# Twelve projection groups multiply activations and their remainders in one 512-column product, and ScalarE and VectorE add the two halves

## The reference, cut to what matters

```python
h = _rmsnorm(x, g_mix[l])
(sb_q, sb_k, sb_v, ...) = jnp.split(h @ w_in[l], offsets, axis=-1)     # group sbq
...
h = _rmsnorm(x, g_ffn[l])
u = _causal_dwconv(h @ w_up[l], ff_conv_w[l], ff_conv_b[l])            # groups up0 to up10
u_val, u_gate = jnp.split(u, 2, axis=-1)
x = x + (jax.nn.silu(u_gate) * u_val) @ w_down[l]                      # groups down0, down1
```

## Time and profile before

| | |
|---|---|
| median of 3 runs | 995.21 us (995.01 to 996.04) |
| the profiled execution's own time | 997.04 us |
| its span, first to last instruction | 995.2 us |
| mean granted TensorE clock | 0.996 |
| TensorE busy | 983.3 us, 99% of the span |
| VectorE busy | 672.6 us, 68% |
| ScalarE busy | 593.6 us, 60% |
| chain of waits that ended last | 94% TensorE |

### The profile page before, as it was taken

How to read it: one execution, slowest core, us unless ns; L and a number is a source line. 1 busy time by engine, 2 the same in 40 slices (tenths; PEclk the granted TensorE clock), 3 DMA queues, 4 the chain that set the end, 5 groups by cost and what they waited for, 6 DMA issues and landing times.

```text
span 995.2 us, 18822 instructions
## 1 busy us (share of the span) xinstructions
PE 983.3 (99%) x8050; PEld 890.0 (89%) x8050; DVE 672.6 (68%) x896; ACT 593.6 (60%) x829; POOL 25.4 (3%) x26
## 2 busy tenths in 40 slices
PE   8999999999999999999999999999999999999996
PEld 7899987888989999998899999889899999987985
DVE  5675688867755788875556565785695556588565
ACT  7677576574537656654446676537754765654581
POOL 0000000000000000000000003000000000130000
PEclk9999999999999999999999999999999999999999
DMA  8762434656565665557654553553556446534331
GB/s 297 270 200 92 150 115 161 210 170 205 176 193 191 187 192 171 170 169 253 190 156 148 147 173 115 163 158 129 172 168 193 151 118 190 170 129 142 137 128 42
DMA packets 97283, 166.45 MB, mean 167 GB/s; under 512 B 6896, under 2 KB 32240, under 8 KB 96816
## 3 DMA queue, kind: packets, MB, share of 16 engines
q1 hardware_dynamic: 95792, 159.18, 50.7%
q0 software_dynamic: 976, 4.46, 1.3%
q10 hardware_dynamic: 432, 1.62, 0.4%
HBM read 164.19 MB, written 1.05 MB: 166 GB/s over the span
## 4 chain that ended last, share of the span: by engine, by line
PE 94%; DVE 2%; ACT 2%; issue 1%; DMA 1%; SPq 0%; DVEq 0%; ACTq 0%
PE proj L623 14%; PE proj L624 14%; PE proj L625 14%; PE proj L632 13%; PE proj L634 13%; PE proj L633 13%; PE mix L668 1%; PE mix L944 1%; PE mix L693 1%; PE mix L676 1%; PE mix L905 1%; PE mix L893 1%; DMA raw<-in_w_mem_kv 1%; ACT arena L1372 1%; PE mix L701 1%
## 5 line engine op out<-in xcount | busy, mean ns | idle before, releaser
L1532 DVE TENSOR_TENSOR wlo<-raw,whi 128x1024 fp32r<-128x1024 f32 (+2 forms) x304 | 356.6, 1202 | 177.3 <-ACT whi L1067 176.0
L1067 ACT ACTIVATE whi<-raw 128x1024 fp32r<-128x1024 f32 (+2 forms) x304 | 307.3, 1040 | 185.4 <-PE proj L634 81.3
L623 PE MATMUL proj<-act_hi,whi 128*128 128x256 f32 x1064 | 304.0, 286 | 0.5 <-ACT arena L1345 0.5
L624 PE MATMUL proj<-act_lo,whi 128*128 128x256 f32 x1064 | 301.0, 283 | 0.0
L625 PE MATMUL proj<-act_hi,wlo 128*128 128x256 f32 x1064 | 301.0, 283 | 0.0
L623 PEld LDWEIGHTS proj<-act_hi,whi 128*128 128x128 f32 x1064 | 203.2, 191 | 3.0 <-ACT arena L1345 1.4
L624 PEld LDWEIGHTS proj<-act_lo,whi 128*128 128x128 f32 x1064 | 203.3, 191 | 0.5
L625 PEld LDWEIGHTS proj<-act_hi,wlo 128*128 128x128 f32 x1064 | 203.2, 191 | 0.2
L632 PE MATMUL proj<-whi,y_hi 128*128 128x512 f32 (+1 forms) x340 | 133.3, 392 | 1.3 <-DVE wlo L1532 1.3
L634 PE MATMUL proj<-whi,y_lo 128*128 128x512 f32 (+1 forms) x340 | 132.3, 389 | 0.0
L633 PE MATMUL proj<-wlo,y_hi 128*128 128x512 f32 (+1 forms) x340 | 132.3, 389 | 0.0
(11 more groups left out here) (335 smaller groups left out, 1027.4 us busy)
## 6 DMA issues: line engine op xcount, KB each, us to landing
raw<-in_w_in SPq DMA_DIRECT2D x144, 512.0 KB, 4.4
raw<-in_w_up SPq DMA_DIRECT2D x88, 256.0 KB, 4.4
raw<-in_w_out SPq DMA_DIRECT2D x32, 512.0 KB, 3.5
raw<-in_w_down SPq DMA_DIRECT2D x22, 512.0 KB, 5.7
raw<-in_w_mem_k SPq DMA_DIRECT2D x8, 512.0 KB, 4.0
raw<-in_w_o SPq DMA_DIRECT2D x8, 512.0 KB, 3.9
raw<-in_w_mem_v SPq DMA_DIRECT2D x8, 512.0 KB, 4.1
raw<-in_w_mem_kv SPq DMA_DIRECT2D x7, 512.0 KB, 6.7
```

The lines of the kernel that those rows point to most:

```text
L623: mm(o, wh[:, i, wc], hi[:, k0 + i, :], start=begin and j % 2 == 0, stop=False, skip_group_check=True)
L624: mm(o, wh[:, i, wc], lo[:, k0 + i, :], start=False, stop=False, skip_group_check=True)
L1067: fn(whi[c % SPLIT][:, 0:w], raw[c % SLOTS][:, 0:w], ACT.Copy).then_inc(s.w_hi, 1)
L1532: tt(wlo[c % SPLIT][:, 0:w], raw[c % SLOTS][:, 0:w], f32(whi[c % SPLIT][:, 0:w]), ALU.subtract).then_inc(s.w_lo, 1)
```

## The change

`act_hi` and `act_lo` become the two halves of one tensor `act_both`. A new function `project_beside` streams both halves in one product of 512 columns against a block of `whi`, into one whole PSUM bank (columns 0 to 255 take hi by hi, columns 256 to 511 take lo by hi), and then the 256-column product of act_hi with `wlo` into columns 0 to 255. A triple of 256-column products becomes a pair. The two halves are added outside: ScalarE copies the upper half to SBUF (`one_side`), VectorE adds the lower half from PSUM to it (`both_sides`). It applies to sbq, up1 to up9 and hgq0 of both layers. A group now takes four banks: in the up stage `mix` for odd and all of `proj4` for even groups; for sbq and hgq0 their own two banks and `mix` banks 2 and 3. `proj` is now a view of `proj4`. ("..." marks what is left out.)

```diff
+SIDE_UP = tuple(f"up{c}" for c in range(1, FT // 2 - 1))
+SIDES = ((None, "sbq"), *((None, name) for name in SIDE_UP), *((L, "hgq0") for L in range(LAYERS)))
...
-        act_hi = sb("act_hi", [P, KT, SEQ], F32R)
-        act_lo = sb("act_lo", [P, KT, SEQ], F32R)
+        act_both = sb("act_both", [P, 2, KT, SEQ], F32R)
+        act_hi, act_lo = act_both[:, 0, :, :], act_both[:, 1, :, :]
...
-        proj = [ctx.enter_context(nc.psum_tensor(f"proj{i}", [P, NB, 512], F32)) for i in range(2)]
+        proj4 = ctx.enter_context(nc.psum_tensor("proj4", [P, 2 * NB, 512], F32))
+        proj = [proj4[:, NB * i:NB * i + NB, :] for i in range(2)]
...
+        def beside(name, L=None):
+
+
+            if name in SIDE_UP:
+                return [(mix if int(name[2:]) % 2 else proj4)[:, j, :] for j in range(4)]
+            return [bank(name, L)[:, 0, :], bank(name, L)[:, 1, :], mix[:, 2, :], mix[:, 3, :]]
...
+        FX = [ar(3072 + n * 1024, 4, SEQ) for n in range(2)]
...
+            def project_beside(name, L):
+
+                ps, at, out = shape[L, name], number[L, name], beside(name, L)
+                k0 = 0
+                for n, loads in enumerate(ps):
+                    pe.wait_ge(s.w_lo, at[n] + 1)
+                    k, cols = piece_dims(loads)
+                    wh = whi[at[n] % SPLIT][:, 0:k * cols].rearrange("p (k c) -> p k c", c=cols)
+                    wl = wlo[at[n] % SPLIT][:, 0:k * cols].rearrange("p (k c) -> p k c", c=cols)
+                    for j in range(4):
+                        wc = slice(j * P, (j + 1) * P)
+                        for i in range(k):
+                            begin, end = k0 + i == 0, k0 + i == KT - 1
+                            mm(out[j].rearrange("p (v t) -> p v t", v=2), wh[:, i, wc], act_both[:, :, k0 + i, :], start=begin, stop=False, skip_group_check=True)
+                            last = mm(out[j][:, 0:SEQ], wl[:, i, wc], act_hi[:, k0 + i, :], start=False, stop=end, skip_group_check=True)
+                    last.then_inc(s.w_used, 1)
+                    k0 += k
...
             project("xaq", None, act_hi, act_lo)
-            project("sbq", None, act_hi, act_lo)
+            pe.wait_ge(*out_of("xav", None))
+            project_beside("sbq", None)
 
             project("sbk", None, act_hi, act_lo, part=(0, 1))
             pe.wait_ge(s.xa_n, 1)
+            pe.wait_ge(*out_of("sbq", None))
...
             project("up0", None, act_hi, act_lo, ready=lambda k: pe.wait_ge(s.ffn_lo, k))
-            for c in range(1, FT // 2):
-                project(f"up{c}", None, act_hi, act_lo)
+            pe.wait_ge(*stage(6, None))
+            for c in range(1, FT // 2 - 1):
+                for name in ("memv",) if c == 1 else ("up0",) if c == 2 else (f"up{c - 2}",):
+                    pe.wait_ge(*out_of(name, None))
+                project_beside(f"up{c}", None)
+            project(f"up{FT // 2 - 1}", None, act_hi, act_lo)
             project("down0", None, y_hi, y_lo, ready=lambda k: pe.wait_ge(s.ff_l, (k + 1) // 2))
...
-                project("hgq0", L, act_hi, act_lo)
+                pe.wait_ge(*out_of("memout0", L))
+                project_beside("hgq0", L)
...
+            def one_side(to, name, L):
+
+                split_until(pieces_until(name, L))
+                act.wait_ge(*done(name, L))
+                if name in SIDE_UP:
+                    v = (mix if int(name[2:]) % 2 else proj4)[:, :, :]
+                    fn(to, v[:, :, SEQ:512], ACT.Copy).then_inc(s.side_in, 1)
+                else:
+                    for v, j in ((bank(name, L), 0), (mix[:, 2:4, :], 2)):
+                        last = fn(to[:, j:j + 2, :], v[:, :, SEQ:512], ACT.Copy)
+                    last.then_inc(s.side_in, 1)
...
-            leave("sbq", None, SBQK[:, 0:4, :])
+            one_side(SBQK[:, 0:4, :], "sbq", None)
...
             def hidden_gate(c):
-                act.wait_ge(*out_of(f"up{c}", None))
+                act.wait_ge(s.ff_v, c + 1)
                 fn(FU[c % 2][:, 2:4, :], FU[c % 2][:, 2:4, :], ACT.Silu).then_inc(s.ff_s, 1)
...
                 if c:
                     hidden_gate(c - 1)
                 split_until(pieces_until(name, None))
-                act.wait_ge(*done(name, None))
+                if name in SIDE_UP:
+                    one_side(FX[c % 2], name, None)
+                if c:
+                    hidden_upper(c - 1)
+                if name in SIDE_UP:
+                    act.wait_ge(*out_of(name, None))
+                else:
+                    act.wait_ge(*done(name, None))
                 if c >= 2:
                     act.wait_ge(s.ff_m, c - 1)
                 for j in range(4):
                     t = 2 * c + j % 2 + FT * (j // 2)
-                    last = fn(FU[c % 2][:, j, :], tiles(name)[:, j, :], ACT.Identity, scale=cols2[:, 2, t:t + 1], bias=cols2[:, 3, t:t + 1])
+                    x = FX[c % 2][:, j, :] if name in SIDE_UP else tiles(name)[:, j, :]
+                    last = fn(FU[c % 2][:, j, :], x, ACT.Identity, scale=cols2[:, 2, t:t + 1], bias=cols2[:, 3, t:t + 1])
                 last.then_inc(s.ff_c, 1)
-                if c:
-                    hidden_upper(c - 1)
...
+            def both_sides(to, name, L):
+
+                dve.wait_ge(s.side_in, SIDES.index((L, name)) + 1)
+                signal = out_of(name, L)[0]
+                if name in SIDE_UP:
+                    v = (mix if int(name[2:]) % 2 else proj4)[:, :, :]
+                    tt(to, v[:, :, 0:SEQ], to, ALU.add).then_inc(signal, 1)
+                else:
+                    for v, j in ((bank(name, L), 0), (mix[:, 2:4, :], 2)):
+                        last = tt(to[:, j:j + 2, :], v[:, :, 0:SEQ], to[:, j:j + 2, :], ALU.add)
+                    last.then_inc(signal, 1)
...
             split_until(pieces_until("sbq", None))
+            both_sides(SBQK[:, 0:4, :], "sbq", None)
             split_until(pieces_until("sbk", None))
...
                 if c:
                     hidden(c - 1)
                 split_until(pieces_until(name, None))
+                x = tiles(name)
+                if name in SIDE_UP:
+                    x = FX[c % 2]
+                    both_sides(x, name, None)
+                if c:
+                    hidden_lower(c - 1)
                 dve.wait_ge(s.ff_c, c + 1)
                 for d in (1, 2):
                     for j in range(4):
                         t = 2 * c + j % 2 + FT * (j // 2)
                         u = FU[c % 2][:, j, d:SEQ]
-                        last = stt(u, tiles(name)[:, j, 0:SEQ - d], cols2[:, 2 - d, t:t + 1], u, ALU.mult, ALU.add)
+                        last = stt(u, x[:, j, 0:SEQ - d], cols2[:, 2 - d, t:t + 1], u, ALU.mult, ALU.add)
                     if d == 1:
                         link(last)
-                last.then_inc(out_of(name, None)[0], 1)
-                if c:
-                    hidden_lower(c - 1)
+                last.then_inc(s.ff_v, 1)
+                if name not in SIDE_UP:
+                    dve.wait_ge(s.ff_v, c + 1)
+                    nc.vector.memset(stat[:, 245:246], 0.0).then_inc(out_of(name, None)[0], 1)
...
-                for name in ("hgq0", "uqa", "uqb", "uk", "uv"):
+                split_until(pieces_until("hgq0", L))
+                both_sides(HQT[:, 0:4, :], "hgq0", L)
+                for name in ("uqa", "uqb", "uk", "uv"):
                     split_until(pieces_until(name, L))
```

6 lines of the change are left out of this document (5 added, 1 removed).

## The result

The changed kernel takes 1008.94 us (median of 4 runs, 1008.18 to 1009.95) against 995.11 us of the kernel before on the same chip (4 runs): ratio 1.014, 95% interval 1.0125 to 1.0155. It is 13.8 us slower. The forecast was +12.7 us, 1007.9 us.

The account below looks back on a forecast made before the run. TensorE, busy 983.3 of 995.2 us, was taken to bound the kernel. Up stage +6.4, sbq +5.4, hgq0 -0.85 and clock +1.75 gave +12.7 us on 995.21, so 1007.9 us; 8-in-10 range 1002 to 1013.

Parts of the forecast that it names:

- What bounds the kernel: Whole kernel: TensorE, busy 983.3 of 995.2 us with no slack, so its work and waits set the time.
- sbq: QK transposes: TensorE waits 5.8 us for sums behind VectorE's four splits; +5.4 us net, bounds 5.2 and 5.6.
- The clock: At the sbq wait: idle TensorE falls to its lower clock once; +1.75 us, bounds 0 and 3.5.
- Rival (1): Whole kernel: the forecast without a fall of the clock, 1006.2 us; chance 0.27.
- rival (4): Up stage: waits of 1.66 us set the clock back too, 47 us over five groups, 1055 us; chance 0.05.
- The up stage: Up groups and down0: VectorE and ScalarE fall behind TensorE once the lead is gone; +6.4 us, bounds 3.4 and 7.6.
- the turn of 12.75 us: Up stage: ScalarE and VectorE's chain from SiLU to SiLU, without overlap, against TensorE's 11.09 us; range 12.35 to 12.9.
- TensorE's gain: Twelve changed groups: pairs of 0.3465 us replace triples of 0.360 us, saving 0.43 us a group, 5.2 us in all.
- hgq0: Both layers' hgq0: no wait or some 0.3 us, so -0.85 us in all, bounds -0.85 and 0.
- The sum: Whole kernel: up stage, sbq, hgq0 and clock terms add to +12.7 us, 1007.9 us; chance 0.55.
- rival (2): Whole kernel: up loop and sbq's sum stay hidden, so TensorE's 5.2 us are gained, 990.0 us; chance 0.05.
- (3): Up stage: turn of 11.4 us or less, covered by the lead, sbq wait as forecast; 997.6 us; chance 0.08.

Follow-up runs that it names:

- e6: Kernel of e2 with sbq's copy and sum moved ahead of the four splits, no instruction more or less; 995.54 us against 995.96, ratio 1.0.
- e8: Instructions of e1 in another order: VectorE's sum first, splits beside scale and bias, SiLU and rounding; 993.88 us against 995.96 before, ratio 0.9973.
- e2: The change in sbq alone, up groups and hgq0 as in the kernel before; 1000.79 us against 995.3, ratio 1.0054.
- e1: The change in up1 to up9 alone, sbq and hgq0 as in the kernel before; 1002.81 us against 995.3, ratio 1.0071.
- e5: Kernel of e2 plus 38 unread 256-column products ahead of the QK transposes, keeping TensorE busy; 1001.52 us against 995.96 before, ratio 1.0054.
- e4: The change in up1 to up3 alone, all other groups as in the kernel before; 995.09 us, ratio 0.9995.
- e11: Kernel of e9 with a piece's products grouped by width, 512, 512, 256, 256; 990.64 us against 995.52 before, ratio 0.9958.
- e3: The change in hgq0 of both layers alone, other groups as in the kernel before; 994.14 us against 995.3, ratio 0.9986.
- e9: All twelve groups changed, with the orders of e6 and e8 and the activation halves side by side; 992.8 us against 996.26 before, ratio 0.9969.

## Why the prediction was right, and which terms were off

**What bounds the kernel**: right. The two profiled spans differ mainly by what TensorE was made to wait, by its clock and by its products, and e6 and e8, which change nothing but places in two queues, move the whole kernel by 5.2 and 8.9 us against e2 and e1 (differences of the medians; 5.4 and 9.8 us by the ratios).

**sbq: +5.4 us forecast, +4.6 measured.** The mechanism is shown (e2, e6). The size was off by how early VectorE reached its splits, 0.7 us in this execution; the forecast took 58.38 from one execution and bounded the term at 5.2, as if that start were exact.

**The clock: +1.75 us forecast, +1.68 measured**, and +1.64 in e2. That the fall would come was right; that its size fits so well is in part luck. It was taken from the kernel's first products, and the profile grants these a clock of 1.00 (window 1.19 to 7.60 us), so that no row shows them slowed by the clock. Nor had the clock "stayed at the upper level" in the trace of before: near 178 us it fell while TensorE was busy (last section), which the slices of rows 1 hide. Rival (1), the same without a fall, is refuted by the windows. e5 shows in its trace that it goes away when TensorE has work. The Trainium skill ("TensorE: Matmul & The Clock Gate", section "The HAM clock gate") has an idle TensorE set back from 2.4 to 1.2 GHz; the windows agree, with 0.59 and 0.64 after 4.6 us of idleness. The waits of 1.4 to 1.6 us in the up stage, with which rival (4) would have brought 1055 us, left the clock up: 1.00 from 385 to 460 us.

**The up stage: +6.4 us forecast, +8.6 measured. This is the term that was mis-sized**, and the step of it that failed is the turn of 12.75 us. The mechanism holds: the splits in front of the sum, a lead that covers the first groups (e4), the first wait in group 6 instead of 5, then one in each group. The turn is 12.94 us.

The four scale-and-bias steps read SBUF now and take 2.08 us, not the 1.94 that the forecast took over from PSUM; those of up10, which still read PSUM, take 1.91 in the same trace. The taps were allowed to become cheaper from SBUF and didn't: 3.37 against 3.34 us. That makes 0.17 of the 0.19 us a turn, and over the eight turns between the first and the last SiLU 1.5 us. Another 0.4 us arose in the first turn, where ScalarE's copy had to wait 1.55 us for TensorE and VectorE 0.79 us for the copy, since up1 ended 0.4 us later than forecast, about half of it by the dearer pairs; the last 0.3 us are what is left for down0. The forecast's bounds gave the turn 0.4 us of room on the cheaper side and 0.15 on the dearer, too little: the stage cost more than its upper bound of 7.6 us.

The Trainium skill has a table for the place of the source that the forecast didn't use ("VectorE: DVE Perf Modes", section "The TRN2 errata"): it gives ScalarE 224 cycles of fixed cost from SBUF and 172 from PSUM, at 1.2 GHz. An estimate from that page is 0.043 us an instruction, 0.17 us for four; the trace has 0.14. The same table gives VectorE 58 cycles from SBUF and 120 from PSUM, by which eight taps would have become about 0.5 us shorter; the trace shows 0.03 us more, and the measurement decides.

**TensorE's gain: 0.43 us a group forecast, 0.22 measured in sbq and in the up groups** (0.353 us a pair in place of 0.3465), **0.41 in hgq0.** In the changed kernel this cost next to nothing, since VectorE's turn sets the stage there; it was what the reordered kernels lacked (e8: -1.9 us where -3.9 was forecast). The choice for it, two rows measured apart in streams of one width each, carried over to the alternating stream in hgq0 (0.3467) and not in the other ten groups, where grouping by width brings 0.348. No run shows why.

**hgq0: -0.85 us forecast, -0.83 measured** in two traces, and the median of e3 (-1.2 us, -2.3 to -0.4) agrees.

**The sum.** The misses +2.2 in the up stage and -0.8 at sbq have opposite signs, with some tenths elsewhere. So the total is nearer to the truth (+12.7 against +13.8) than its largest term, and that is luck. Rivals (2) and (3), a stage that stays hidden, are refuted for the kernel as it was changed; e11 reached the time of rival (2) with the order changed.

## What to carry to other kernels

When a step is moved off the engine that bounds the kernel, look up what stands in front of it in the other engines' queues: the same copy and sum cost 5.5 us behind four splits and nothing ahead of them (a wait of 1.0 us in e9). Where two engines hand work to each other several times a turn, add up the turn as a chain with the durations of the new operand places (SBUF or PSUM), and put work that nobody waits for into its gaps; a lead hides a turn that is too long only for some groups. And a price per product is good to a few nanoseconds only: the same pairs took 0.347 us in one place of the kernel and 0.353 in another.

## What the runs showed of the hardware, unexpected

**A fall of the clock without idleness.** TensorE of before by time, and windows of before; then the window of after in the same stage, which lies 6.5 us later there:

```profile
176.06 1.97 PE L790 MATMUL mix<-arena,const 4*128 4x256 f32 x8
...
178.00:180.00 2.00, 2.00 (x8) 1.63 (x8) 2.00 (x7) 1.97 (x3) 0.00 (x0) 0.75 0.93 326
180.00:182.00 2.00, 2.00 (x7) 1.51 (x6) 1.26 (x4) 1.99 (x2) 0.00 (x0) 0.50 1.02 392
```

```profile
186.00:188.00 2.00, 2.00 (x11) 1.63 (x10) 1.74 (x6) 1.97 (x3) 0.00 (x0) 1.00 1.03 365
```

TensorE is busy throughout in both (2.00 of 2.00 us), and yet before loses some 1.6 us here: the 40 digits of the page, each a 25 us average, hide it. Just ahead of the fall stand 2 us of products that use 4 of the 128 rows (`4x256`); they stand there in every execution, and the fall follows only in some. Of the 14 profiled executions six have it (before, e3, e4, e5, e6, e11), and these took 0.1 to 2.2 us more than the median of their kernel; the other eight took 0 to 1.7 us less. So it is a likely part of why runs of one kernel lie 2 to 3 us apart, and why this profiled execution took 997.04 us; the forecast took its 1.8 us over the median as mere scatter. What sets it off stays open.

**The same pair of products at two prices**: 512- and 256-column products that follow each other singly take 0.353 us a pair in sbq and in the up stage and 0.347 us in hgq0, in every run that has them. Two and two take 0.348 us in all three places. The cause is open.

**ScalarE from SBUF**: four scale-and-bias steps of 256 columns take 2.08 us from SBUF and 1.91 to 1.94 us from PSUM, while VectorE's taps of 255 columns take the same from both (3.37 and 3.34 us for eight).
